# Two projections of a short convolution as seven block products, their sums on GpSimd, in a two-block network on one NeuronCore

## The chip, the core and the metric

The program runs on 1 core of one Trainium2 chip. The metric is the device time of one execution in microseconds (us). All data is float32. The engines are called by their names in the profile: PE (TensorE, matmuls) and PEld (its weight loads), DVE (VectorE), ACT (ScalarE), POOL (GpSimd), and SP, whose queue issues the weight loads from HBM. Every engine takes its instructions in the order in which they are written; semaphores order the engines among each other.

## The reference

Two blocks run one after the other. The first is a stack of two layers over 16 meta tokens and 256 real ones (272 tokens of width 1024); the second is a larger block that the change does not touch. The part of a layer that the change touches is the mixer, which projects the normalised tokens `u` with one matrix and splits the result:

```python
u = rms_norm(h, pre_g)
z = jnp.einsum("bld,de->ble", u, w_in)
q, k, v, f_logit, a_val, a_gate, sc_b, sc_c, sc_x = jnp.split(z, idx, axis=-1)
log_f = jax.nn.log_sigmoid((f_logit + b_forget).astype(jnp.float32))
y_attn = forgetting_attention(q, k, v, log_f)          # 8 heads of 64
a = a_val * jax.nn.sigmoid(a_gate)
a = causal_depthwise_conv(a, a_dw_w) + a_dw_b          # 31 taps, 256 channels
a = jax.nn.silu(layer_norm(a, a_ln_g, a_ln_b))
y_conv = jnp.einsum("blc,ce->ble", a, a_pw_w)
y_sc = sc_b * causal_depthwise_conv(sc_c * sc_x, sc_conv_w)   # 3 taps, 256 channels
y = jnp.concatenate([y_attn, y_conv, y_sc], axis=-1)
y = jnp.einsum("ble,ed->bld", head_rms_norm(y, head_g), w_out)
```

After it comes the layer's feed-forward network (FFN).

## The kernel before

Activations lie feature-major: 128 features on the partitions, 272 tokens beside each other, eight such tiles for the width of 1024 (`U` holds `u`). Weights come in strips of 1024 rows by 256 columns (1 MB), one after the other through four slots `W[0]` to `W[3]` in a written order. SP loads a strip into a slot when PE has signalled `done` of the slot's last strip; PE waits for `land` of the slot. Results are made in eight PSUM banks of 512 columns; a bank is taken with `take(b)` and freed by the engine that has read it.

In a layer's mixer PE goes through a fixed list: strips of `a_val` and `a_gate`, the query, forget and key strips, the first value strip (`values(0, i)` in three pieces), scores of heads 0 and 1 (`scores(j)`, two matmuls), the two statistics of the layer norm behind the 31-tap convolution (`stat(CV, ...)`, which waits for the semaphore `conv`, and `stat(SQ, ...)`; line 786), then the strips of `sc_c` (slot 1, in two halves, `half_slot`, line 1089), `sc_x` (slot 2, `slot_fm`, line 806), the second value strip, `sc_b`, and so on. Between them stand the transposes of the weighted scores (`turn(j)`, line 1107), the next scores (lines 1096, 1097), and the products of weights and values (`weigh(pair)`).

A strip by `slot_fm` or `half_slot` is two output tiles of eight matmuls each: 128x128 weights, 272 tokens. ACT copies each finished tile to SBUF. In float32 each written matmul is two instructions of PE in the trace.

DVE computes the 31-tap convolution of the mixer in the same time as PE runs the query, key and value strips: for each tap and each of the two channel tiles one instruction (line 2996 for the first tap, line 2998 for the other 30), with both inputs in SBUF. Behind tap 9 stand the three small instructions of the forget gate. Behind the convolution DVE takes the row minima of the scores (`mask_min`, line 3005), the mean subtraction of the layer norm, and reciprocals (`invert`), all in that order.

POOL fills constants, and in a layer's mixer it zeroes the query and key tiles (line 1842), sets ones in them (line 1912), issues two small DMAs behind the forget gate (lines 1918, 1919), copies a diagonal (line 1924), and then waits for reciprocals from DVE to scale exponentials (lines 1926, 1931, 1933).

The FFN of a layer, further on, already computes its strips by seven block products (`seven_products`, line 852): of a strip seen as 2x2 blocks (two output tiles, two halves of the 1024 rows) and the tokens as 2x2 blocks (two halves of the rows, two halves of 136 tokens), seven products of sums of blocks take the place of eight. Each product is four matmuls over 136 tokens. The sums of tokens are made once by DVE, the sums of weights for each strip by POOL (lines 1943, 1945) and DVE. ACT takes snapshots of unfinished results (line 2057), which DVE adds to the rest (lines 2949, 2953, 2959).

`p.meet` and `p.leave` only carry semaphore counts from one engine's program to another's.

## Time and profile before

| | before |
|---|---|
| time, median of 3 runs | 1957.62 us (1957.46 to 1958.21) |
| span of the profiled execution | 1956.5 us |
| instructions in it | 31965 |
| PE busy | 1935.6 us (99%) |
| DVE busy | 1276.0 us (65%) |
| ACT busy | 576.3 us (29%) |
| POOL busy | 219.5 us (11%) |
| PE's share of the chain that ended last | 94% |

The span goes from the first to the last instruction of the profiled execution; the medians of the runs stand 1.1 us above it (1957.62 - 1956.5), which is what lies around the instructions. Times in rows are microseconds from the start of the span. A timeline row is: start, duration, engine, line, operation, output<-inputs, shape, count, and in brackets the idle time of the engine before it with what ended it. Consecutive instructions of one line are merged into one row. The granted clock of PE is shown as PEclk, where 1.00 is 2.4 GHz and 0.50 is 1.2 GHz; it stands at 0.9 or more in all 40 slices of the page.

### The profile page before, as it was taken

To read this page: it belongs to the slowest core of one execution; us is meant where nothing else is said; L and a number is where in the kernel's file an instruction comes from. 1 tells how busy PE (TensorE), PEld (TensorE's weight loads), DVE (VectorE), ACT (ScalarE), POOL (GpSimd) and SP (SyncE) were. 2 spreads that over 40 slices of the span, in tenths; PEclk is the share of its full clock that TensorE was granted. 3 is DMA by queue.
4 is the path that set the end of the run, shared out by engine and by line. 5 is a ranking of instruction groups with operands and counts; after the bars stand their busy time and mean duration, and the time that the engine had idled before them with its cause. 6 is when DMAs were issued, how large, how long until landed. Compare 5 with 4: busy or idle time off the path is not lost.

```text
span 1956.5 us, 31965 instructions
## 1 busy us (share of the span) xinstructions
PE 1935.6 (99%) x12809; PEld 1755.3 (90%) x12809; DVE 1276.0 (65%) x2559; ACT 576.3 (29%) x1393; POOL 219.5 (11%) x267
## 2 busy tenths in 40 slices
PE   9999999999999999999999999999999999999998
PEld 7878999977799999888888887999998999999998
DVE  5425887572278865899768556445566776766664
ACT  3343332224533313111110003433343323132211
POOL 6100440312014200000000001001211200000000
PEclk9999999999999999999999999999999999999999
DMA  6354554353545542555545355332222224545552
GB/s 207 109 193 133 165 168 155 121 152 118 171 151 166 190 136 74 180 166 167 172 159 175 103 174 169 104 107 87 87 65 70 82 75 142 172 151 165 165 172 82
DMA packets 272109, 273.85 MB, mean 140 GB/s; under 512 B 7982, under 2 KB 269338, under 8 KB 271962
## 3 DMA queue, kind: packets, MB, share of 16 engines
q1 hardware_dynamic: 270152, 267.84, 42.9%
q0 software_dynamic: 1216, 3.32, 0.5%
q8 instruction: 102, 1.67, 0.4%
q10 hardware_dynamic: 594, 0.65, 0.1%
q14 instruction: 45, 0.37, 0.1%
HBM read 270.57 MB, written 1.08 MB: 139 GB/s over the span
## 4 chain that ended last, share of the span: by engine, by line
PE 94%; DVE 3%; ACT 1%; DMA 1%; issue 1%; ACTq 0%; DVEq 0%; SPq 0%; PEldq 0%
PE bank L852 53%; PE bank L806 8%; PE bank L1367 8%; PE bank L1586 5%; PE bank L1003 2%; PE bank L1452 2%; PE bank L1637 2%; PE bank L1730 1%; PE bank L1080 1%; PE bank L1570 1%; PE bank L1130 1%; PE bank L1692 1%; PE bank L1089 1%; PE bank L1433 1%; PE bank L1284 1%; PE bank L1278 1%
## 5 line engine op out<-in xcount | busy, mean ns | idle before, releaser
L852 PE MATMUL bank<-arena,SQ 128*128 128x136 f32 (+2 forms) x2176 | 341.4, 308 | 0.1
L852 PEld LDWEIGHTS bank<-arena,SQ 128*128 128x128 f32 x2176 | 307.0, 191 | 17.2 <-ACT arena L2057 0.3
L852 PE MATMUL bank<-arena,W 128*128 128x136 f32 (+2 forms) x1824 | 272.6, 301 | 2.7 <-issue 2.1
L852 PEld LDWEIGHTS bank<-arena,W 128*128 128x128 f32 x1824 | 247.6, 191 | 15.3 <-issue 4.1
L2057 ACT ACTIVATE H<-bank 128x128 f32<-128x128 f32 (+1 forms) x260 | 82.4, 317 | 534.3 <-PE bank L852 534.2
L852 PE MATMUL bank<-U,W 128*128 128x136 f32 (+2 forms) x1296 | 194.6, 303 | 0.0
L852 PEld LDWEIGHTS bank<-U,W 128*128 128x128 f32 x1296 | 176.4, 191 | 10.9 <-issue 2.9
L3205 DVE SCALAR_TENSOR_TENSOR W<-W,CC 128x256 f32<-128x256 f32 x280 | 128.3, 483 | 7.0
L852 PE MATMUL bank<-arena 128*128 128x136 f32 (+1 forms) x1024 | 124.1, 278 | 0.0
L852 PEld LDWEIGHTS bank<-arena 128*128 128x128 f32 x1024 | 120.6, 191 | 0.0
L806 PE MATMUL bank<-U,W 128*128 128x272 f32 (+1 forms) x512 | 118.4, 392 | 1.4 <-ACT U L2355 0.8
L806 PEld LDWEIGHTS bank<-U,W 128*128 128x128 f32 x512 | 96.8, 190 | 22.1 <-issue 2.3
L2057 ACT ACTIVATE arena<-bank 128x136 f32<-128x136 f32 x176 | 49.3, 280 | 169.3 <-PE bank L852 169.2
L852 PE MATMUL bank<-U,SQ 128*128 128x136 f32 (+2 forms) x608 | 98.2, 304 | 0.0
L852 PEld LDWEIGHTS bank<-U,SQ 128*128 128x128 f32 x608 | 85.9, 191 | 4.1
L1943 POOL TENSOR_TENSOR SQ<-W 128x512 f32<-128x512 f32 x32 | 40.8, 1275 | 268.7 <-PE bank L852 268.7
L1988 POOL TENSOR_TENSOR W<-W 128x512 f32<-128x512 f32 x32 | 42.1, 1316 | 250.4 <-PE bank L1637 105.8
L3104 DVE SCALAR_TENSOR_TENSOR arena<-arena,PL 128x270 f32<-128x270 f32 x72 | 61.8, 859 | 2.6
L1963 POOL DMA_DIRECT2D gate_rows<-arena x4 | 2.1, 542 | 528.0 <-ACT arena L2451 528.0
L2263 ACT ACTIVATE arena<-arena,PL 128x272 f32<-128x272 f32 x80 | 41.8, 522 | 64.4 <-DVE arena L2953 56.9
L852 PE MATMUL bank<-arena,U 128*128 128x256 f32 (+1 forms) x352 | 59.2, 327 | 0.4 <-DVE U L2936 0.4
L1586 PE MATMUL bank<-H,W 128*128 128x256 f32 x256 | 59.1, 380 | 0.3 <-ACT W L2545 0.3
(505 smaller groups left out, 3266.8 us busy)
## 6 DMA issues: line engine op xcount, KB each, us to landing
W<-in_ffn_w_up_dram SPq DMA_DIRECT2D x44, 1024.0 KB, 5.1
W<-in_ffn_w_in_dram SPq DMA_DIRECT2D x44, 1024.0 KB, 5.1
W<-in_ada_w_dram SPq DMA_DIRECT2D x36, 1024.0 KB, 7.1
W<-in_mix_w_in_dram SPq DMA_DIRECT2D x36, 1024.0 KB, 5.4
W<-in_ffn_w_down_dram SPq DMA_DIRECT2D x16, 1408.0 KB, 7.0
W<-in_ffn_w_out_dram SPq DMA_DIRECT2D x16, 1408.0 KB, 6.4
W<-in_w_in_dram SPq DMA_DIRECT2D x21, 1024.0 KB, 6.0
W<-in_w_out_dram SPq DMA_DIRECT2D x8, 1024.0 KB, 8.7
```

Source lines behind the costliest of these rows:

```text
L806: last = mm(bank[b][0:m, 0:n], W[r][:, kk, t * P:t * P + m], rhs(kk), start=kk == 0, stop=kk == k - 1)
L852: last = mm(o, a(k), b[:, k], start=not adds and k == 0, stop=k == kt - 1, skip_group_check=True)
L1003: return mm(bank[2 * (r % 2) + t][:, c0:c0 + n], W[r][:, k, t * P:(t + 1) * P], rhs(k), start=k == 0, stop=k == KD - 1, skip_group_check=True)
L1367: last = mm(o, x, y, start=i == 0, stop=i == n - 1 and bias is None, skip_group_check=True)
L1452: last = mm(bank[b][:, c + n * P:c + (n + 1) * P], tok[:, k, n * P:(n + 1) * P], w[:, k], start=clear and k == n == 0, stop=k == 3, skip_g ...
L1586: ins = mm(o, x, y, start=clear and k == 0, stop=k == 3, skip_group_check=True)
L1943: eng.tensor_tensor(WS[n % 2][:, 0], part(1, 0), part(1, 1), ALU.add).then_inc(S.order_pool, p.inc(S.order_pool))
L1988: eng.tensor_tensor(WSR[o], x, y, op).then_inc(S.wsum, p.inc(S.wsum))
L2057: act(sn[:, i, :], bank[b][:, c:c + w], ACT.Copy).then_inc(S.snap, p.inc(S.snap))
L2263: act(CZ[:, 2 * s + t, :], Z[:, g % 2, 2 * s + t, :], ACT.Copy, scale=PLs[l][:, c:c + 1]).then_inc(S.tap, p.inc(S.tap))
L3104: stt(CZ[:, i, 2:], Z[:, g % 2, i, 0:T1 - 2], w(0), CZ[:, i, 2:], ALU.mult, ALU.add).then_inc(sem, p.inc(sem))
L3205: ins = stt(o, x, c, o, ALU.mult, ALU.add) if k else ts(o, x, c, None, ALU.mult)
```

## The change

It touches the mixer of both layers. The strips of `sc_c` and `sc_x` are computed by seven block products (`mixed_steps`), like the FFN's strips but in two banks rather than three: both halves of a 512-column bank serve as separate accumulators. The sums that they need are all written for POOL: four sums of token blocks (`TBM_`, 128x544 each) behind the setting of ones, and four sums of weight blocks (128x512 each) for each of the two strips behind the copy of the diagonal. ACT takes four snapshots of 136 columns for each strip in place of two copies of 272 (`kept_mixed`), and DVE adds them to what the banks hold at the end (`mixed_fold`), behind the reciprocals of heads 2 and 3. ACT's SiLUs of the convolution branch, with the two table loads around them, move from behind `exps(3)` to behind `mixed(0)`, the copy of the first pair of weighted values. The pointwise weights are loaded by two DMAs into the last rows of slots 0 and 1 rather than by one into slot 0. Several semaphores are merged into `kept` and `cact`; that changes no wait.

```diff
+        TBM_ = [v[:, 4 * i:4 * i + 4, c:c + T1 // 2] for v, c in ((U, 2 * P + 32), (SQ, T1)) for i in range(2)]
+        WSA = TBU
+        WSB = [H2[:, 4 * (i // 2):4 * (i // 2) + 4, (i % 2) * P:(i % 2 + 1) * P] for i in range(4)]
+        SNM = HIB[:, SEQ:SEQ + 2 * T1].rearrange("p (i n) -> p i n", i=4)
...
-                eng.dma_start(W[0][:, KD:KD + 2, :], cols(pw, 0, k=2)).then_inc(S.land[0], p.inc(S.land[0], 16))
+                for k in range(2):
+                    eng.dma_start(W[k][:, SK - 1:SK, :], cols(pw, 0, k0=k, k=1)).then_inc(S.land[0], p.inc(S.land[0], 16))
...
+                def mixed_steps(r, o):
...
+                    eng.wait_ge(S.land[r], p.next(S.land[r], 16))
+                    take(bx)
+                    for k in range(4):
+                        add(bank[bx][:, near], raw(0, 0, k), layer_tokens(0, 0)[:, k], k, True)
+                        yield
+                    take(by)
+                    if r == 1:
+                        eng.wait_ge(S.mix_tsum, p.next(S.mix_tsum))
+                    eng.wait_ge(S.mix_wsum, p.next(S.mix_wsum))
+                    for k in range(4):
+                        add(bank[by][:, near], o[0][:, k], TBM_[0][:, k], k, True)
+                        yield
+                    eng.wait_ge(S.mix_snap, p.next(S.mix_snap))
+                    for k in range(4):
+                        add(bank[bx][:, far], raw(0, 1, k), layer_tokens(1, 0)[:, k], k, False, False)
+                        yield
+                    eng.wait_ge(S.mix_snap, p.next(S.mix_snap))
+                    for k in range(4):
+                        add(bank[by][:, far], raw(1, 1, k), TBM_[3][:, k], k, False)
+                        yield
...
+                    eng.wait_ge(S.mix_wsum, p.next(S.mix_wsum))
+                    eng.wait_ge(S.mix_snap, p.next(S.mix_snap))
+                    for k in range(4):
+                        ins = add(bank[bx][:, near], o[2][:, k], TBM_[2][:, k], k, False)
...
-                half_slot(1, 0)
+                multipliers = mixed_steps(1, WSA)
+                weave(multipliers, 16)
                 turn(0)
                 scores(2)
-                half_slot(1, 1)
+                weave(multipliers, None)
                 turn(1)
                 scores(3)
-                slot_fm(2, u1, T1)
+                weave(mixed_steps(2, WSB), None)
                 turn(2)
...
+            def mixed_sums(r, o, loads):
+
+                part = lambda t, h: W[r][:, 4 * h:4 * h + 4, t * P:(t + 1) * P]
+                eng.wait_ge(S.land[r], p.next(S.land[r], loads))
+                for i, x, y, op in ((0, part(1, 0), part(1, 1), ALU.add), (1, o[0], part(0, 0), ALU.subtract),
+                                    (3, part(0, 1), o[1], ALU.subtract), (2, part(0, 0), part(1, 0), ALU.subtract)):
+                    eng.tensor_tensor(o[i], x, y, op).then_inc(S.mix_wsum, p.inc(S.mix_wsum))
+                    eng.wait_ge(S.mix_wsum, p.now(S.mix_wsum))
...
+                eng.wait_ge(S.us, p.next(S.us, KD))
+                p.skip(S.us, KD)
+                for n, x, y in ((0, layer_tokens(0, 1), layer_tokens(0, 0)), (1, layer_tokens(1, 1), TBM_[0]),
+                                (2, layer_tokens(1, 1), layer_tokens(0, 1)), (3, layer_tokens(1, 0), TBM_[1])):
+                    sem = S.mix_tsum if n == 3 else S.order_pool
+                    eng.tensor_tensor(TBM_[n], x, y, ALU.subtract).then_inc(sem, p.inc(sem))
+                    eng.wait_ge(sem, p.now(sem))
                 eng.wait_ge(S.f_ready, p.next(S.f_ready))
...
+                p.meet(f"mixed{l}")
+                mixed_sums(1, WSA, 32)
+                mixed_sums(2, WSB, 32)
                 eng.wait_ge(S.rc, p.next(S.rc))
...
+                def kept_mixed(r, which):
...
+                    for n in which:
+                        i, src = ((0, x), (3, z), (1, x), (2, y))[n]
+                        eng.wait_ge(S.mix_prod, p.next(S.mix_prod, 2 if n == 2 else 1))
+                        act(SNM[:, i, :], src, ACT.Copy).then_inc(S.mix_snap, p.inc(S.mix_snap))
...
+                kept_mixed(1, (0, 1))
                 evict(0)
+                kept_mixed(1, (2,))
                 exps(2)
-                copies(1, SCC)
+                kept_mixed(1, (3,))
                 evict(1)
                 exps(3)
+                kept_mixed(2, range(4))
+                evict(2)
+                exps(4)
+                mixed(0)
                 for t in range(2):
                     eng.wait_ge(S.xn, p.next(S.xn))
                     act(CS[:, t, :], CV[:, t, :], ACT.Silu, bias=PLs[l][:, C_LNB + t:C_LNB + t + 1]).then_inc(S.cact, p.inc(S.cact))
                 if l == 0:
                     act(CC[:, :, 6:8], GS[:, 0, :, :], ACT.Silu).then_inc(S.cc, p.inc(S.cc))
                 tables(LOG_EXP)
-                copies(2, SCX)
-                evict(2)
-                exps(4)
-                mixed(0)
                 values(3, 1)
...
+                def mixed_fold(r, dst):
...
+                    eng.wait_ge(S.mix_snap, p.next(S.mix_snap, 4))
+                    tt(dst[:, 0, far], SNM[:, 1, :], bank[by][:, near], ALU.add).then_inc(S.order_dve, p.inc(S.order_dve))
...
+                    eng.wait_ge(S.mix_prod, p.next(S.mix_prod, 6))
+                    tt(dst[:, 0, near], SNM[:, 0, :], bank[bx][:, far], ALU.add)
...
                     invert(j % 3, 2)
+                    if j in (2, 3):
+                        r, dst = {2: (1, SCC), 3: (2, SCX)}[j]
+                        mixed_fold(r, dst)
```

The first place is POOL's program in a layer's mixer. Before, behind the zeroing of the arena tiles (`QA`, `KA`, `QC`), it stands so:

```order
L1842 MEMSET arena 128x16
L1912 AFFINE_SELECT arena<-arena 8x4x272 x2
L1918 DMA arena<-arena 8x4x272
L1919 DMA arena<-arena 8x4x272
L1924 COPY arena<-arena 128x8x16
L1926 TENSOR_SCALAR arena<-arena,RC 128x272
```

With the change the same place reads so; `U` and `SQ` hold the token sums, `W` and `H` (H2) the weight sums:

```order
L1969 AFFINE_SELECT arena<-arena 8x4x272 x2
L1978 TENSOR_TENSOR U<-U 128x4x136 x2
L1978 TENSOR_TENSOR SQ<-U 128x4x136 x2
L1982 DMA arena<-arena 8x4x272
L1983 DMA arena<-arena 8x4x272
L1988 COPY arena<-arena 128x8x16
L1957 TENSOR_TENSOR W<-W 128x512 x4
L1957 TENSOR_TENSOR H<-W 128x4x128
L1957 TENSOR_TENSOR H<-H,W 128x4x128
L1957 TENSOR_TENSOR H<-W,H 128x4x128
L1957 TENSOR_TENSOR H<-W 128x4x128
L1993 TENSOR_SCALAR arena<-arena,RC 128x272
```

Twelve instructions with two SBUF inputs have been set ahead of the scaling of exponentials, four of them ahead of the two DMAs. DVE's program in the same part of a layer is the same as before: the convolution is L2998 before and L3080 with the change, between the gate's `FM` and `FC` (8x272) and the first row minima.

The second place is PE's program from the first layer's score matrices over the strips of `sc_c` and `sc_x`. Before, with the convolution's statistic as the rows of `mean_c`:

```order
L786 MATMUL bank<-arena,mean_c 128x272 x2
L1080 MATMUL bank<-W,U 128x256 x8
L786 MATMUL bank<-SQ,mean_c 128x272 x2
L1074 MATMUL bank<-W,U 32x256 x8
L1165 MATMUL bank<-ident,arena 128x128 x2
L1167 MATMUL bank<-ident,arena 32x128 x4
L1089 MATMUL bank<-U,W 128x272 x8
L1107 MATMUL bank<-ident,arena 128x128 x3
L1096 MATMUL bank<-arena 128x128
L1097 MATMUL bank<-arena 128x256
L1089 MATMUL bank<-U,W 128x272 x8
```

With the change, from the first strip's first product on:

```order
L1102 MATMUL bank<-U,W 128x136 x12
L1102 MATMUL bank<-SQ,W 128x136 x4
L1158 MATMUL bank<-ident,arena 128x128 x3
L1147 MATMUL bank<-arena 128x128
L1148 MATMUL bank<-arena 128x256
L1102 MATMUL bank<-U,W 128x136 x8
L1102 MATMUL bank<-SQ,W 128x136 x4
```

Four products (16 matmuls) stand ahead of the first transposes and three (12) behind the next scores, where two output tiles of eight matmuls over 272 tokens stood. Everything ahead of the strip is in the same order.

## Rows read from the trace of the kernel before

**Rows 1.** The page, busy time and share by engine.

```profile
PE 1935.6 (99%) x12809; PEld 1755.3 (90%) x12809; DVE 1276.0 (65%) x2559; ACT 576.3 (29%) x1393; POOL 219.5 (11%) x267
```

**Rows 2.** Timeline of PE, first layer: start us, duration us, instruction, count.

```profile
66.90 1.08 PE L786 MATMUL bank<-arena,mean_c 128*128 128x272 f32 x4
...
74.00 3.93 PE L1089 MATMUL bank<-U,W 128*128 128x272 f32 x16
...
82.42 0.49 PE L1107 MATMUL bank<-ident,arena 128*128 128x128 f32 x3
...
83.41 7.50 PE L806 MATMUL bank<-U,W 128*128 128x272 f32 x32
```

**Rows 3.** Timeline of PE, second layer.

```profile
438.43 1.08 PE L786 MATMUL bank<-arena,mean_c 128*128 128x272 f32 x4
```

**Rows 4.** Timeline of DVE, first layer.

```profile
46.68 19.97 DVE L2998 SCALAR_TENSOR_TENSOR arena<-arena,PL 128x272 f32<-128x272 f32 x42
...
83.61 0.29 DVE L3005 CUSTOM_DVE_ANT_0 arena<-bank,mask 128x128 f32<-128x128 f32 x1 [2.67 <-PE bank L1097]
```

**Rows 5.** Timeline of DVE, second layer.

```profile
405.62 0.92 DVE L2981 TENSOR_TENSOR arena<-arena 128x272 f32<-128x272 f32 x2 [0.88 <-ACT arena L2103]
...
417.45 20.11 DVE L2998 SCALAR_TENSOR_TENSOR arena<-arena,PL 128x272 f32<-128x272 f32 x42
```

**Rows 6.** Timeline of ACT, first layer.

```profile
75.37 0.38 ACT L2140 ACTIVATE arena<-bank 128x256 f32<-128x256 f32 x1
...
85.09 0.18 ACT L2153 ACTIVATION_READ_ACCUMULATOR arena<-arena,NM 128x1 f32 x1
```

**Rows 7.** Timeline of PE, FFN of the first layer.

```profile
190.74 2.02 PE L852 MATMUL bank<-U,W 128*128 128x136 f32 x16
192.59 2.02 PE L852 MATMUL bank<-arena,SQ 128*128 128x136 f32 x16
```

**Rows 8.** The page's groups: count, busy us, mean ns of one, idle before.

```profile
L2057 ACT ACTIVATE arena<-bank 128x136 f32<-128x136 f32 x176 | 49.3, 280 | 169.3 <-PE bank L852 169.2
```

**Rows 9.** Timeline of ACT, second layer.

```profile
472.52 0.60 ACT L2139 ACTIVATE arena<-bank 128x512 f32<-128x512 f32 x1 [7.12 <-PE bank L1074]
```

**Rows 10.** Timeline of POOL, first layer.

```profile
34.36 2.44 POOL L1912 TENSOR_SCALAR_AFFINE_SELECT arena<-arena 8x1088 f32<-8x1088 f32 x2
```

**Rows 11.** Timeline of SP's queue, 52 to 55 us.

```profile
53.74 0.37 SPq L592 DMA_DIRECT2D W<-in_w_in_dram  x1
```

**Rows 12.** DMA issues: source, count, size each, median us from issue to landing.

```profile
W<-in_w_in_dram SPq DMA_DIRECT2D x21, 1024.0 KB, 6.0
```

**Rows 13.** Timeline of POOL, FFN of the first layer.

```profile
204.05 1.27 POOL L1943 TENSOR_TENSOR SQ<-W 128x512 f32<-128x512 f32 x1 [3.69 <-PE bank L852]
205.40 1.35 POOL L1945 TENSOR_TENSOR SQ<-W 128x512 f32<-128x512 f32 x1
210.53 1.27 POOL L1943 TENSOR_TENSOR SQ<-W 128x512 f32<-128x512 f32 x1 [3.79 <-PE bank L852]
```

**Rows 14.** Timeline of DVE, the same stretch.

```profile
204.56 1.06 DVE L3101 SCALAR_TENSOR_TENSOR arena<-arena,PL 128x271 f32<-128x271 f32 x1
205.66 1.39 DVE L3104 SCALAR_TENSOR_TENSOR arena<-arena,PL 128x270 f32<-128x270 f32 x1
207.08 0.50 DVE L3101 SCALAR_TENSOR_TENSOR arena<-arena,PL 128x271 f32<-128x271 f32 x1
...
211.12 0.44 DVE L2959 TENSOR_TENSOR arena<-arena,bank 128x272 f32<-128x272 f32 x1
```

**Rows 15.** Timeline of DVE, 35.8 to 36.1 us.

```profile
35.74 1.35 DVE L2998 SCALAR_TENSOR_TENSOR arena<-arena,PL 128x272 f32<-128x272 f32 x1
```

**Rows 16.** Timeline of PE, end of the program.

```profile
1949.67 0.42 PE L1812 MATMUL bank<-ident,arena 128*128 128x128 f32 x2
```

**Rows 17.** Windows: us, busy of PE, PEld, DVE, ACT, POOL, PEclk, DMA share, GB/s.

```profile
1953.00:1956.50 3.50, 0.00 (x0) 0.00 (x0) 0.00 (x0) 0.00 (x0) 0.00 (x0) 0.55 0.74 276
```

**Rows 18.** Timeline of PE, start of the program.

```profile
2.84 4.61 PE L757 MATMUL bank<-ident 128*128 128x128 f32 x20 [2.84 <-POOL LNT L1851]
```

More of the change, by code:

```diff
@@ L1186, in _ @@
                 scores(5)
-                eng.wait_ge(S.land[0], p.next(S.land[0], 16))
+                eng.wait_ge(S.land[0], p.next(S.land[0], 32))
                 slot_fm(0, u1, T1)
@@ L2212, in _ @@
                 exps(5)
[L2213 removed]
+                copies(0, SCB, S.kept)
                 evict(4)
```

83 lines of the change are left out of this document (55 added, 28 removed).

## The prediction

> **What bounds the kernel now.** I read the page first: PE is busy 99% of the span, DVE 65%, POOL 11% [rows 1]. PE's one long pause is the first 2.84 us of the program [rows 18]. So every microsecond of work that PE loses is a microsecond of time, and any wait that another engine puts in front of PE costs as much, unless there is slack. Then I laid the timelines of PE, DVE and POOL around the two strips beside each other. In the first layer PE comes to the first statistic of the convolution (`stat(CV)`) at 66.90 [rows 2], and DVE's last 42 taps run from 46.68 for 19.97 us, to 66.65 [rows 4]. The convolution is done 0.25 us before PE asks for it. In the second layer PE comes at 438.43 [rows 3] and the taps end at 417.45 + 20.11 = 437.56 [rows 5]: 0.87 us. PE shows no wait there, and yet DVE's convolution is all but critical: it runs some 30 us without a pause under PE's strips. Everything that follows on DVE (row minima, layer norm, reciprocals) stands behind it.
>
> **The strips themselves.** A strip before is 32 instructions of PE over 272 tokens (16 written matmuls) and lasts 7.50 us with the drain of the last [rows 2]. Seven products of four matmuls over 136 tokens are 56 instructions. The FFN runs them already: 16 last 2.02 us, but the next begins after 192.59 - 190.74 = 1.85 [rows 7], so the drain is 0.17 and the pace 0.116 each. A strip goes from 7.50 - 0.17 = 7.33 us to 56 x 0.116 = 6.48. The gain is 0.85 us a strip, 3.4 us for four.
>
> The snapshots give part of that back. The third product may begin only when ACT has copied the first. In the first strip PE starts at 74.00 [rows 2] and is through two products at 75.85. ACT is busy with the value copies until 75.37 + 0.38 = 75.75 [rows 6], then needs 0.28 for a snapshot [rows 8] and, my estimate, 0.15 for two handovers: PE goes on at about 76.2, a wait of 0.35. In the second strip, count from the first transpose behind the first strip (82.42 before). PE begins the strip 83.41 - 82.42 = 0.99 us later and wants the first snapshot 1.85 us after that, at 2.84; ACT ends `exps(3)` at 85.09 + 0.18, which is 2.85 [rows 2, 6], and the snapshot is there at about 3.2: again 0.35. DVE's folds do not add to this: `mask_min(3)` begins 83.61 - 82.42 = 1.19 us after the transpose [rows 2, 4], and the three adds of a fold fit ahead of it. Two waits of 0.35 in each of two layers are 1.4 us. The strips are worth 3.4 - 1.4 = 2.0 us.
>
> The moved SiLUs cost nothing: they and their two table loads land in a stretch in which ACT sits idle for 7.12 us ahead of the second value copy [rows 9]. If that cover were too short, `evict(3)` and with it the transposes of head 4 would be late next. The second DMA for the pointwise weights costs nothing: the rows that it fills are free, and the wait for slot 0 comes behind the second value strip.
>
> **The sums on POOL, and what they meet.** When do the twelve run? In the first layer POOL is done with line 1912 at 34.36 + 2.44 = 36.8 [rows 10], so the four token sums run from there, some 6 us. The strip of `sc_x` is issued at 53.74 [rows 11], that of `sc_c` one strip of 7.33 us before, at 46.4, and each lands some 6.0 us later [rows 12]: POOL makes their sums from about 52.5 to 58.5 and from 59.7 to 65.7. All twelve lie between 36.8 and 66.65, under the convolution. In the second layer the first token sum can start as soon as `U` is written, which is before DVE's pause of 0.88 us ahead of 405.62 [rows 5]; the other eleven meet line 2981 or the taps behind it. POOL itself has the time: its next instruction, the first scaling, needs a reciprocal that DVE makes only behind the convolution.
>
> What does DVE pay for a tensor operation of POOL beside it? The FFN shows it. POOL's two sums start at 204.05 and 205.40 [rows 13]. DVE's `scalar_tensor_tensor` instructions, of the same kind as the taps, last 0.50 us alone, 1.06 beside the first sum and 1.39 beside the second; from start to start it is 205.66 - 204.56 = 1.10 and 207.08 - 205.66 = 1.42 [rows 14], where alone it would be 0.53 (0.50 and the handover). So a sum of 128x512 costs DVE 0.57 us where DVE comes upon it midway and 0.89 where both queue without a pause. The taps are not exempt: the one that starts at 35.74 lasts 1.35 us [rows 15], beside line 1912 on POOL [rows 10], where the later ones come every 19.97 / 42 = 0.475 us [rows 4]. In the mixer both engines queue without a pause, so I take 0.89 for each weight sum and, scaled by 544/512, 0.95 for each token sum. First layer: 8 x 0.89 + 4 x 0.95 = 10.9 us. Second layer, with three token sums, the first of them in part in DVE's own pause (0.3 us less, an estimate): 8 x 0.89 + 3 x 0.95 - 0.3 = 9.7 us.
>
> The Trainium skill, page "SBUF — State Buffer", section "Who interferes with whom", speaks against this change: a DVE instruction with two SBUF inputs contends with a GpSimd instruction that reads SBUF, and the one that comes second is blocked until the other is through. The trace agrees in kind (1.39 us in place of 0.50) but shows less than the 1.27 us that the sum lasts. Taken to the letter, the rule gives the time of the second rival below.
>
> PE cannot cover it. Its list puts `stat(CV)` ahead of the next value pieces, so it stands still for 10.9 - 0.25 = 10.65 us in the first layer and for 9.7 - 0.87 = 8.8 us in the second, 19.5 us together. What is behind the statistic (minima, exponentials, transposes) keeps its distances and only shifts.
>
> **The clock.** PE has no pause of this length within its work. But behind its last matmul, at 1949.67 + 0.42 = 1950.09 [rows 16], the granted clock falls: its mean over 1953.00 to 1956.50 is 0.55 [rows 17], so it was full for the first 0.35 us and half (1.2 GHz) for the rest, and fell 3.3 us after the work ended. A pause of 9 to 11 us should then end at the lower clock. What that costs is seen at the start: 20 instructions over 128 columns last 4.61 us, 0.23 each [rows 18], where 136 columns take 0.116 later [rows 7]. Half of 4.61 is lost, 2.3 us, and I take that for each pause: 4.6 us. The bounds are 0 (the clock stays) and twice that.
>
> **The sum.** 1957.6 - 2.0 (strips) + 19.5 (pauses) + 4.6 (clock) = 1979.7 us. It is made on the span of the profiled execution (1956.5, so 1978.6 with the change) and carries over to the median, which lies 1.1 us above that span.
>
> **Rivals.**
> - *The convolution is not held up*: only the strips count, 1955.6 us, or 1954.2 without the snapshot waits. For it: beside the sum at 210.53 an add of 272 columns with one input in PSUM lasts its plain 0.44 us [rows 13, 14], so the two engines can live together, and no row shows a tap beside a tensor operation of POOL. Against it: the taps have both inputs in SBUF, like the instructions that were held up. This is the rival on the other side; it needs the loss for each sum to stay under (0.25 + 0.87 + 2.0) / 23, about 0.14 us. 8%.
> - *A sum holds DVE for its whole length*: 23 x 1.28 = 29.4, less the slack of 1.1, gives 28.3; 1957.6 - 2.0 + 28.3 + 4.6 = 1988.5 us. For it: both queues are denser than anywhere in the trace. Against it: 0.89 at the densest place there is. 15%.
> - *Only the lighter price*: each sum costs 0.57, as the first of the FFN's pair. 23 x 0.57 - 1.1 = 12.0 us of pauses, each longer than 3.3: 1957.6 - 2.0 + 12.0 + 4.6 = 1972.2 us. 13%.
> - *The clock stays at full*: 1957.6 - 2.0 + 19.5 = 1975.1 us. 12%.
> - *The forecast* as summed, within 1975.5 and 1985: 52%.
>
> **How the numbers follow.** Faster by over 0.2% means under 1953.7 us, slower by over 0.2% over 1961.5; that is about what a measurement of this kernel can tell from no change. The first rival falls between the two almost wholly (0.06), with 0.02 for faster; all others are slower, 0.92. The range leaves out the first rival and reaches from below the light price to the full block: 1970 to 1989.
>
> **What the profile of the changed kernel would show.** If right: most taps still last 0.50 us, but about 22 of the 120 last 1.3 to 1.5 us, each beside a sum on POOL; the taps end near 77.5 and 447 us; PE waits for DVE at `stat(CV)`, some 10.6 and 8.8 us, its two longest waits; PEclk falls to 0.5 behind each of them. The strips: 56 instructions of about 0.116 us, with two waits for ACT's snapshots of 0.2 to 0.5 us in each layer. If the taps end by 67 and 438 us, the step that failed is the price of a sum on DVE; if PE waits but resumes at full pace, it is the clock; if the waits within the strips are above 1 us, it is the snapshots. The forecast is wrong as a whole if POOL's sums run outside the convolution.

## The result: 1986.2 us, 1.4% slower

The changed kernel takes 1986.19 us (median of 4 runs, 1983.52 to 1988.67) against 1957.72 us (1957.46 to 1958.21) for the kernel before: ratio 1.0144, 95% interval 1.013 to 1.0159. The forecast was 1979.7 with a range of 1970 to 1989. The profiled execution of the changed kernel is the longest of its four, 1988.67 us with a span of 1986.9; the spread of 5 us over these four, where the four of the kernel before spread over 0.75, will need a reason too.

The page of the changed kernel, busy time by engine, beside [rows 1]:

```profile
PE 1941.8 (98%) x12905; PEld 1762.8 (89%) x12905; DVE 1302.4 (66%) x2571; ACT 576.5 (29%) x1401; POOL 251.7 (13%) x291
```

PE has 96 matmuls more and DVE 26 us more of busy time, though its 12 added instructions are short: it was made to wait inside its own instructions. What PE waited for (us in total, times, longest):

```profile
PE bank L792 <- DVE arena L3080: 20.2, 2, 11.2
PE bank L1400 <- DVEq L3310: 4.7, 4, 2.2
PE bank L763 <- POOL LNT L1899: 2.8, 1, 2.8
```

The first line is the statistic of the convolution, foreseen. The second, in the second block, was not. The third stands in the kernel before as well. PE's timeline around the strips, first layer (line 1102 is the products), beside [rows 2]:

```profile
78.18 2.15 PE L792 MATMUL bank<-arena,mean_c 128*128 128x272 f32 x4 [11.25 <-DVE arena L3080]
80.13 5.44 PE L1090 MATMUL bank<-W,U 128*128 128x256 f32 x16
...
88.14 3.46 PE L1102 MATMUL bank<-U,W 128*128 128x136 f32 x24
91.44 1.09 PE L1102 MATMUL bank<-SQ,W 128*128 128x136 f32 x8
92.36 0.49 PE L1158 MATMUL bank<-ident,arena 128*128 128x128 f32 x3
...
103.00 1.09 PE L1102 MATMUL bank<-SQ,H 128*128 128x136 f32 x8
103.93 0.27 PE L1158 MATMUL bank<-ident,arena 128*128 128x128 f32 x1
```

and in the second layer, beside [rows 3]:

```profile
460.45 2.15 PE L792 MATMUL bank<-arena,mean_c 128*128 128x272 f32 x4 [8.93 <-DVE arena L3080]
```

DVE's last 42 taps, first layer and second, beside [rows 4, 5]:

```profile
50.66 27.79 DVE L3080 SCALAR_TENSOR_TENSOR arena<-arena,PL 128x272 f32<-128x272 f32 x42
...
433.17 27.54 DVE L3080 SCALAR_TENSOR_TENSOR arena<-arena,PL 128x272 f32<-128x272 f32 x42
```

POOL's sums in the first layer (four of tokens, eight of weights):

```profile
36.85 2.83 POOL L1978 TENSOR_TENSOR U<-U 128x544 f32<-128x544 f32 x2 [0.18 <-POOL arena L1969]
39.76 2.92 POOL L1978 TENSOR_TENSOR SQ<-U 128x544 f32<-128x544 f32 x2
...
53.19 5.53 POOL L1957 TENSOR_TENSOR W<-W 128x512 f32<-128x512 f32 x4
58.90 1.26 POOL L1957 TENSOR_TENSOR H<-W 128x512 f32<-128x512 f32 x1 [0.19 <-DMA W<-in_w_in_dram]
```

The reader is to see three things. POOL's sums run where they were placed, 36.85 to 64.4, all under the convolution. Four of them push the start of the last 42 taps from 46.68 to 50.66, 3.98 us or 1.00 each; eight more stretch those taps from 19.97 to 27.79, 7.82 us or 0.98 each (second layer 27.54 - 20.11 = 7.43, 0.93 each). Instruction by instruction, 99 of the 120 taps last about 0.5 us. The other 21 last 1.35 to 1.77 us: the first of them beside line 1969 of POOL, as in the kernel before [rows 15], and 20 beside a sum. The four token sums of the second layer end at 422.6, ahead of its first tap (423.1): they meet the two instructions of line 3063 and the two of 3078, which take 2.82 and 1.65 us, where the kernel before has 0.92 and 0.75. And the four matmuls of the statistic take 2.15 us where [rows 2] has 1.08. Windows (columns as in [rows 17], PEclk third from the end) say why:

```profile
78.20:83.80 5.60, 5.60 (x13) 4.42 (x14) 3.07 (x16) 3.23 (x12) 1.64 (x3) 0.50 0.01 3
85.40:92.00 6.60, 6.46 (x60) 4.86 (x59) 1.00 (x2) 2.92 (x9) 0.92 (x1) 1.00 0.51 159
461.00:466.00 5.00, 5.00 (x13) 3.90 (x12) 2.54 (x15) 3.23 (x12) 1.58 (x3) 0.50 0.01 3
```

(The first two numbers of a window row are its ends, in us; then come its length and the busy time of PE, PEld, DVE, ACT and POOL.) Behind each pause PE works at half its clock (1.2 GHz), from 78.18 to 83.8 and from 460.45 to 466.1, and then at full again.

**The account.** Where an unchanged instruction of PE starts in the two traces, first behind both layers, then through the second block:

```
before us   after us   later by
   855.9      879.8      23.82
   880.9      906.0      25.08
   905.8      931.7      25.92
   931.2      957.8      26.54
   933.7      963.9      30.23
  1949.8     1980.3      30.49
```

The two layers cost 23.8 us: 20.2 of pauses, 5.7 of clock, less 1.9 for the strips (a sum of 24.0). Another 6.7 us are lost between 880 and 966 us, in code that the change does not touch. PE waits there for sums that DVE makes of modulation weights, 4.7 us in four waits, and DVE is late because it waits for a weight strip of the FFN (DVE and PE, the same turn of that loop):

```profile
871.66 0.69 DVE L2969 TENSOR_TENSOR SQ<-W 128x512 f32<-128x512 f32 x1 [1.75 <-DMA W<-in_ffn_w_in_dram]
...
881.34 0.64 PE L1400 MATMUL bank<-W,ONE 128*32 128x256 f32 x8 [1.19 <-DVEq L3310]
```

Most of the rest is the clock once more. Behind the last and longest of the four waits it is at half from 961.0 to 964.4, and 16 matmuls take 5.41 us where the kernel before takes 3.72, 1.7 us more. PE's timeline and a window of the changed kernel, and the same matmuls before:

```profile
960.32 0.64 PE L1400 MATMUL bank<-W,ONE 128*32 128x256 f32 x8 [2.19 <-DVEq L3310]
960.89 5.41 PE L862 MATMUL bank<-U,W 128*128 128x256 f32 x16
```
```profile
961.00:964.40 3.40, 3.40 (x9) 2.65 (x10) 3.04 (x5) 0.00 (x0) 0.00 (x0) 0.51 0.90 294
```
```profile
932.09 3.72 PE L852 MATMUL bank<-U,W 128*128 128x256 f32 x16
```

These 6.7 us are those of the profiled execution, which is 2.5 us above the median of the four; in the others the second block may well lose less.

### The profile page after: what moved, and what is told of

It is laid out like the page before. It is cut to its first block, busy times and chain, and to the rows that moved or that the text cites. A ratio compares the mean times of both kernels' runs of the same rounds, so it can differ in the third digit from the quotient of the medians.

```text
span 1986.9 us, 32217 instructions
## 1 busy us (share of the span) xinstructions
PE 1941.8 (98%) x12905; PEld 1762.8 (89%) x12905; DVE 1302.4 (66%) x2571; ACT 576.5 (29%) x1401; POOL 251.7 (13%) x291
## 3 DMA queue, kind: packets, MB, share of 16 engines
HBM read 270.57 MB, written 1.08 MB: 137 GB/s over the span
## 4 chain that ended last, share of the span: by engine, by line
PE 85%; DVE 10%; DMA 2%; ACT 2%; issue 1%; DVEq 0%; POOL 0%; ACTq 0%; POOLq 0%
PE bank L862 48%; PE bank L1419 8%; PE bank L816 5%; PE bank L1638 4%; DVE arena L3080 4%; PE bank L1013 2%; PE bank L1504 2%; PE bank L1689 2%; PE bank L1181 1%; PE bank L1778 1%; PE bank L1622 1%; DVE W L3306 1%; DMA W<-in_ffn_w_in_dram 1%; PE bank L1090 1%; PE bank L1744 1%; PE bank L1102 1%
## 5 line engine op out<-in xcount | busy, mean ns | idle before, releaser
L862 PEld LDWEIGHTS bank<-U,W 128*128 128x128 f32 x1296 | 177.6, 191 | 11.5 <-issue 2.9
L816 PE MATMUL bank<-U,W 128*128 128x272 f32 (+1 forms) x448 | 103.4, 392 | 1.4 <-ACT U L2437 0.8
L816 PEld LDWEIGHTS bank<-U,W 128*128 128x128 f32 x448 | 84.6, 190 | 19.6 <-issue 2.3
L3080 DVE SCALAR_TENSOR_TENSOR arena<-arena,PL 128x272 f32<-128x272 f32 x120 | 75.3, 669 | 2.1
```

The lines of the kernel that those rows point to most:

```text
L816: last = mm(bank[b][0:m, 0:n], W[r][:, kk, t * P:t * P + m], rhs(kk), start=kk == 0, stop=kk == k - 1)
L862: last = mm(o, a(k), b[:, k], start=not adds and k == 0, stop=k == kt - 1, skip_group_check=True)
L3080: ins = stt(CV[:, t, :], src, w, CV[:, t, :], ALU.mult, ALU.add)
```

## The experiments

Eleven kernels. The reasons to test were: a sum of POOL holds DVE up when both read SBUF; the clock is a cost of its own; the strips are worth 2 us; and for the 6.7 us a theory that is set out behind the fourth run. The kernel before ran again beside them (1957.59, 1957.63 and 1957.94 us), and each ratio is to it.

### Without the sums

POOL makes none of its twelve sums; PE's products read raw blocks in their place (the last one the identity), so that the two projections are not those of the reference.

```diff
-                    eng.tensor_tensor(o[i], x, y, op).then_inc(S.mix_wsum, p.inc(S.mix_wsum))
+                    eng.sem_inc(S.mix_wsum, p.inc(S.mix_wsum))
...
-                        add(bank[by][:, near], o[0][:, k], TBM_[0][:, k], k, True)
+                        add(bank[by][:, near], raw(1, 0, k), layer_tokens(0, 1)[:, k], k, True)
```

> The twelve tensor operations of POOL in each layer's mixer are left out (POOL only signals); the seven products read unsummed blocks of weights and tokens (the last one the identity), so the two projections are not those of the reference. Everything else is the changed kernel. Theory A (POOL's sums hold up DVE's taps, PE waits for the convolution, and its clock falls): the taps end near 66.7 and 437.5 us, PE has no wait at the statistic, and only the strips count: 1957.7 - 2.0 = 1955.7 us, within 1954 to 1957. Rival B (the loss lies in the strips themselves, their snapshots, folds or bank waits): it stays near 1986. Rival C (the second block lost some 7 us through something the change did to the loads, not through the delay): some 1962 us.

1959.67 us (1958.68 to 1963.34, 10 runs), ratio 1.0014 (1.0005 to 1.0023). PE's timeline:

```profile
67.11 1.08 PE L792 MATMUL bank<-arena,mean_c 128*128 128x272 f32 x4
...
74.22 4.38 PE L1102 MATMUL bank<-U,W 128*128 128x136 f32 x32
...
90.01 0.49 PE L1158 MATMUL bank<-ident,arena 128*128 128x128 f32 x3
```

No wait at the statistic, no half clock, and the two strips with what lies between last 90.01 - 74.22 = 15.79 us, as in the changed kernel (103.93 - 88.14 = 15.79). Pauses and clock hang on the sums. But the kernel does not come out below the one before, as was expected: PE is 2.2 us ahead of it at the entry of the second block and 1.4 behind at the end, so the second block loses 3.6 us, most of it at the same line 1400.

### The sums, with plain strips

The opposite half: POOL makes all sums, PE computes `sc_c` and `sc_x` with `half_slot` and `slot_fm`.

```diff
-                multipliers = mixed_steps(1, WSA)
-                weave(multipliers, 16)
+                eng.wait_ge(S.mix_tsum, p.next(S.mix_tsum))
+                eng.wait_ge(S.mix_wsum, p.next(S.mix_wsum, 4))
+                half_slot(1, 0)
...
-                weave(mixed_steps(2, WSB), None)
+                eng.wait_ge(S.mix_wsum, p.next(S.mix_wsum, 4))
+                slot_fm(2, u1, T1)
```

> POOL's twelve sums in each layer stay, at the same places, and PE waits for them, but the two strips are again eight plain products over 272 tokens, with ACT's copies and without DVE's folds. Theory A: the same two pauses of 11.2 and 8.9 us at the statistic and the same clock loss of some 5.7 us; the strips no longer give their 2 to 3 us: 1957.7 + 20.2 + 5.7 = 1983.6, plus what the second block loses (0 to 7 us, as it falls), so 1984 to 1990. Rival B: 1958 to 1962.

1982.92 us (1981.52 to 1984.02), ratio 1.0129 (1.0114 to 1.0144). What PE waited for at the statistic:

```profile
PE bank L792 <- DVE arena L3091: 20.2, 2, 11.2
```

The same 20.2 us to the digit, so the products do not make the pauses. The program is 24.0 us later at the end and as late already ahead of the second block, which loses nothing; the expectation of at least 1984 lay above the time because it added a clock loss of 5.7 us, where 4.4 were lost (6.70 + 6.42 - 2 x 4.37). Oddly, a kernel with the slower strips is faster than the changed one, by 6.5 us on the spans of the profiled executions (1986.9 against 1980.4) and 3.3 by the medians. The spans: 6.7 us of the second block, and 1.3 of the clock (from the first statistic to the second PE takes 6.70 and 6.42 us here, 7.23 twice in the changed kernel and 4.37 in the one before), less 1.9 for the strips, 6.1 of the 6.5. At the entry of the second block the two kernels stand within 0.2 us of each other (23.8 and 24.0 us behind the kernel before), and one loses 6.7 us there and the other nothing: the delay as such is not what costs.

### Writes in place of sums

Plain strips again, and each sum of POOL is two `memset` of the same tile: POOL is busy in the same places and only writes.

```diff
-                    eng.tensor_tensor(o[i], x, y, op).then_inc(S.mix_wsum, p.inc(S.mix_wsum))
+                    eng.memset(o[i], 0.0).then_inc(S.order_pool, p.inc(S.order_pool))
+                    eng.wait_ge(S.order_pool, p.now(S.order_pool))
+                    eng.memset(o[i], 0.0).then_inc(S.mix_wsum, p.inc(S.mix_wsum))
```

> As plain_strips, but each sum of POOL is replaced by two memsets of the same place, which write SBUF and read nothing, so POOL is busy about as long in the same stretch. Theory A in its narrow form (what holds DVE's two-input instructions up is that POOL reads SBUF): no tap lasts over 0.6 us beside a memset, no pause, 1957 to 1959 us. Rival D (any work of POOL on SBUF holds DVE up): a loss in proportion to POOL's busy time, 1970 to 1990 us.

1957.45 us (1956.83 to 1957.86, 10 runs), ratio 0.9999 (0.999 to 1.0009). DVE's last 42 taps, and one of POOL's writes beside them:

```profile
46.40 19.94 DVE L3096 SCALAR_TENSOR_TENSOR arena<-arena,PL 128x272 f32<-128x272 f32 x42
```
```profile
53.22 0.52 POOL L1972 MEMSET W<- 128x512 f32 x1
```

No tap is held up (19.97 us in [rows 4]). What costs is not POOL's writing, nor its instructions or semaphores; what the sums do beyond that is read SBUF. Reads without writes were not tried.

### The clock kept up

38 matmuls of 128 columns ahead of each statistic, where PE stands still anyway.

```diff
+                take(7)
+                keep_busy(bank[7][:, 0:P], 38)
+                eng.sem_inc(S.free[7], 1)
                 stat(CV, T1, True, 2, b=7, ready=S.conv, full=S.ln_full, lhs=mean_c)
```

> The changed kernel with 38 extra matmuls of 128 columns on PE, into the bank of the statistic, ahead of the statistic in each layer: some 8.4 us of work at full clock, which fits into the pauses of 11.25 and 8.93 us. Theory A: the pauses as such stay, the clock does not fall, and the 2.85 + 2.8 us that PE ran at half pace come back: 5.7 us less than the changed kernel, about 1980.5. Rival E (the clock falls anyway, or costs nothing): no change. If the second block's loss is a matter of when its loads land, it will change by some microseconds with the shift, in either direction.

1977.89 us (1977.73 to 1978.89), ratio 1.0103 (1.0086 to 1.012). PE's timeline and a window (columns as above):

```profile
69.90 8.65 PE L803 MATMUL bank<-mean_d,ident 128*128 128x128 f32 x76
80.25 1.16 PE L792 MATMUL bank<-arena,mean_c 128*128 128x272 f32 x4 [1.70 <-DVE arena L3083]
```
```profile
80.00:86.00 6.00, 5.75 (x32) 4.68 (x36) 3.34 (x17) 3.41 (x13) 1.76 (x3) 1.00 0.00 0
```

The clock stays full, and the statistic is followed by the strip after 87.43 - 80.25 = 7.18 us, where the changed kernel takes 88.14 - 78.18 = 9.96 and [rows 2] 7.10. The half clock costs the changed kernel 2.86 us a pause (9.96 - 7.10). This kernel is 8.3 us faster than the changed one by the medians and 9.7 by the spans. Of these, 5.6 are the clock (9.96 - 7.18 = 2.78 in the first layer and as much in the second) and 6.7 the second block, which loses nothing here; some 2.6 are given back, 2.1 of them ahead of the first statistic (80.25 against 78.18), where the clock was at half from 9.9 to 16.7 us. Why would the second block lose nothing?

### The theory of the fetches

Queue 8 of the profile carries instructions (the other such queue, 14, has packets of another size). Its line on the page of the changed kernel:

```profile
q8 instruction: 103, 1.69, 0.4%
```

103 packets of 16 KB; PE has 2 x 12905 = 25810 instructions with its weight loads, so one packet for each 250, and with the 568 that its sequencer handles alone (waits and increments, by the trace) 26378, one for each 256. Before has 102. In the second block they come some 26 us apart, and the loads of FFN strips that DVE's sums wait for come every 25 to 26 us. Start of each fetch in the second block, from the packets of that queue, and of those loads with the time to landing:

```
kernel            fetches us                     loads us (us to landing)
before            860.8 886.6 911.9 937.9        866.2 (5.13) 891.1 (5.17) 916.5 (5.11) 941.5 (5.26)
after             865.1 891.3 917.9 944.3        865.1 (6.56) 891.3 (6.14) 917.0 (5.84) 943.1 (7.55)
no_sums           839.2 865.5 891.4 917.5        839.0 (6.64) 865.3 (5.64) 890.6 (5.64) 916.4 (6.88)
plain_strips      859.6 884.7 910.0              865.2        890.2        915.1        (all about 5.0)
keep_clock        856.5 881.4 908.2 933.1        861.9 (5.21) 886.9 (5.07) 911.8 (4.94) 937.2 (4.97)
```

In `after` and `no_sums` the fetch falls on the issue of the load or up to 1.2 us behind it, and the load lands 0.5 to 2.4 us late; in the others the fetch starts 3.6 to 5.6 us ahead of it. All 13 traces agree. Between 825 and 975 us they hold 77 such loads with a recorded landing: the 19 with a fetch that starts between issue and landing (0 to 4.3 us behind the issue) land after 5.21 to 7.55 us, 17 of them after more than 5.6, and the other 58 after 4.85 to 5.52. The change adds 192 instructions of PE (96 matmuls, 96 weight loads). The 38 written fillers of a layer add 152, those of both layers 304, so that `keep_clock` has 496 more than the kernel before: nearly two whole distances between fetches, which puts them back beside the loads as before. The theory (F in the expectations): how many instructions PE has run decides on which load a fetch falls; the second block loses where they meet. Its rival is that the content of the change (sums, order, late transfers) reaches into the second block.

### 64 idle increments at the start of the changed kernel

```diff
+            for _ in range(64):
+                eng.sem_inc(S.pad, 1)
             eng.wait_ge(S.consts, p.next(S.consts))
```

> The changed kernel with 64 idle instructions more in PE's program (increments of a semaphore that nobody waits for), at its very start, where PE waits for POOL's constants. In the changed kernel's trace the second block lost 6.7 us because four weight strips (issued at 865.1, 891.3, 917.0 and 943.1) landed after 5.8 to 7.6 us instead of 5.1, and a 16 KB fetch of PE's instructions (queue 8) stands at 865.1, 891.3, 917.9 and 944.3. Theory F (the fetches, one for about every 256 instructions of PE, here some 26 us apart like the strips, fall upon the strips' loads, and the change moved them there with its 192 more instructions): 64 more instructions move each fetch some 6.5 us ahead, between the loads; the second block's waits on DVE go, 1980 to 1981 us, with a narrower spread. Rival G (the loss comes with the seven products or with the shift in time as such): 1984 to 1988 as before.

1984.37 us (1983.6 to 1985.53), ratio 1.0134 (1.0119 to 1.0149). PE's waits:

```profile
PE bank L795 <- DVE arena L3083: 14.3, 2, 8.9
PE bank L766 <- issue: 12.6, 1, 12.6
```

The increments were no idle matter: they begin at 2.7 us and the 64 take 9.7, 0.15 each, so that the first matmul comes at 12.6 and not at 2.8; most of that is taken back at the first statistic, where the wait is 5.3 us and not 11.25. PE enters the second block 1.6 us later than in the changed kernel and loses nothing there (landings 5.04 to 5.25), as F says. The total is 1.8 us below the changed kernel by the medians, 5.1 by the spans, but above the 1980 to 1981 expected: the increments were taken to cost nothing.

### 192 increments where none was lost

The counter-test: plain strips, which had no loss, with the number of instructions that the products add, 96 in each pause.

```diff
+                for _ in range(96):
+                    eng.sem_inc(S.pad, 1)
                 stat(CV, T1, True, 2, b=7, ready=S.conv, full=S.ln_full, lhs=mean_c)
```

> plain_strips (the sums on POOL, the strips as plain products, 1982.9 us, no wait in the second block) with 96 idle instructions of PE in each layer, inside the long pause at the statistic, where they cost nothing: 192 in all, as many as the seven products add. Theory F: the fetches fall upon the loads as in the changed kernel, and the second block loses 3 to 7 us: 1986 to 1990. Rival G: 1982.9.

1991.85 us (1990.29 to 1994.37), ratio 1.0173 (1.0158 to 1.0188). PE's waits:

```profile
PE bank L793 <- issue: 24.8, 2, 12.4
PE bank L1416 <- DVEq L3321: 4.8, 4, 1.3
```

The increments again cost more than the pause holds (PE stands still for 12.4 us each time, in place of 11.2 and 9.0), and the total lies above the 1986 to 1990 expected. But the wait in the second block is there, without a single product: 4.8 us, four times, and PE loses 5.0 us between its entry and its end. Fetches at 872.5 and 898.7 meet loads at 872.4 and 898.5, and two more, at 928.2 and 955.6, start 3.6 and 4.3 us behind loads at 924.6 and 951.3; the four land after 6.42 to 6.72 us. This run carries most for F.

### The sums moved out from under the convolution

All the work of the changed kernel. POOL makes the weight sums behind the convolution, around its first scalings; DVE makes the token sums behind its reciprocals.

```diff
-                mixed_sums(1, WSA, 32)
-                mixed_sums(2, WSB, 32)
+                eng.wait_ge(S.conv, p.next(S.conv, 2))
+                mixed_sums(1, WSA, 32, (0, 1))
...
+                    if j == 1:
+                        mixed_sums(1, WSA, 32, (2, 3))
+                        mixed_sums(2, WSB, 32)
```

> The changed kernel with the sums where DVE has no convolution to run: POOL waits for the end of the convolution and makes two weight sums of the first strip ahead of the first scaling and the other six behind the scalings of heads 0 and 1; DVE makes the four token sums itself behind the reciprocals of heads 0 and 1. The work is the whole of the changed kernel's. Theory A: no pause at the statistic, no fall of the clock, the strips give their 2 us; PE's instruction stream is that of the changed kernel, so by theory F the second block loses what it lost in no_sums, some 3.5 us: about 1959.5. If DVE's token sums meet POOL's scalings and come late, the first strip waits up to 1 us in each layer: up to 1961.5. Rival G would have 1956 to 1958.

1961.23 us (1957.98 to 1964.3, 10 runs), ratio 1.0016 (1.0006 to 1.0025). 25 us of the loss are gone: no pause, no half clock, and the program is 2.1 us ahead of the kernel before at the entry of the second block, which is what the strips bring. The second block gives away 3.1 us; PE's wait:

```profile
PE bank L1400 <- DVEq L3313: 2.9, 3, 1.6
```

With the 64 increments at its start:

> later_sums with the 64 idle instructions of PE at the start of the program. Theories A and F together: no pause, no fall of the clock, no fetch upon the loads: 1957.6 - 2.0 = 1955.6 us, within 1954.5 to 1957.5, and 3 to 4 us below later_sums. Rival G: the same as later_sums.

1965.06 us (1964.48 to 1965.96, 6 runs), ratio 1.0037 (1.0024 to 1.0049). The second block keeps its length (landings 5.04 to 5.22 us), and the six runs lie within 1.5 us of each other, where the ten of `later_sums` lie within 6.3. But nothing takes back what the increments cost: the first statistic comes 8.8 us later (75.56 against 66.76), so that the total missed the 1955.6 expected. A cheaper way to shift the count was needed.

### Narrow matmuls in place of increments

Matmuls of 4 columns behind the warm-up; one written is four instructions of PE.

```diff
+            for _ in range(16):
+                mm(bank[4][0:4, 0:4], ident[:, 0:4], ident[:, 0:4], start=True, stop=True, skip_group_check=True)
```

16 in the changed kernel:

> The kernel after with 16 narrow matmuls (4 columns, 64 more instructions of PE) behind the warm-up at the start. Theory F: the fetches move a quarter of their distance off the loads, the second block keeps its length (no shift beyond that of the two layers), and the kernel is faster than after by 6.7 us less the cost of the narrow matmuls (1 to 3 us): 1980 to 1983 us. Pauses at the statistic and the half clock behind them as in after. Rival: the second block's loss belongs to the change and stays: 1987 to 1989 us.

1981.42 us (1980.33 to 1982.32), ratio 1.0117 (1.0103 to 1.0131). PE's timeline at the start, and the issues of 860 to 950 us in `before`, `after` and this kernel (count, size, median us to landing):

```profile
7.11 0.94 PE L765 MATMUL bank<-ident 128*4 128x4 f32 x32
```
```profile
W<-in_ffn_w_in_dram SPq DMA_DIRECT2D x7, 1024.0 KB, 5.1
```
```profile
W<-in_ffn_w_in_dram SPq DMA_DIRECT2D x7, 1024.0 KB, 6.4
```
```profile
W<-in_ffn_w_in_dram SPq DMA_DIRECT2D x7, 1024.0 KB, 5.0
```

They take 0.9 us and hide ahead of a load: the matmul that waits for it starts at 9.58 us, in the changed kernel at 9.56. Set against the trace of the changed kernel, PE is 1.2 us earlier at the entry of the second block (the two stretches at half clock cost 3.7 us here, from statistic to statistic 5.93 and 6.48) and 7.9 earlier at the end: the 6.7 us of the profiled execution are back, by 64 instructions that compute nothing. By the medians the gain is 4.8 us (1986.19 - 1981.42).

51 in the kernel before, meant to put its own fetches on its loads:

> The kernel before with nothing but 51 narrow matmuls (4 columns, 204 more instructions of PE) behind the warm-up at the start of the program. Theory F (the second block's loss is PE's own instruction fetches falling on the issue of the FFN strips' loads; which load they meet is set by how many instructions PE has run): 204 instructions are 0.8 of the 256 between two fetches, so the fetch at 886.6 comes at about 866, on the load at 866.2, and so do the following ones. The second block, untouched, then loses 3 to 7 us of PE (its waits for DVE at the modulation sums), on top of what the narrow matmuls cost at the start (at 0.02 to 0.1 us for each of 102 instructions 2 to 10 us), which shows in the first block. Rival: the loss in the second block comes from the changed content of the first (another order of DVE or POOL, a late transfer): then the second block keeps its length here to 0.5 us.

1963.44 us (1962.4 to 1965.21, 8 runs), ratio 1.0026 (1.0016 to 1.0037). In the profiled execution 2.8 us are lost ahead of the second block (the matmuls, and an early dip of the clock) and only 1.5 in it, under the 3 that F asked for. The fetches at 869.4, 895.2 and 920.9 meet loads at 869.0, 894.9 and 920.2; these land after 6.27, 5.21 and 5.82 us. The sign is right and the wait at the modulation sums is there:

```profile
PE bank L1350 <- DVEq L3211: 1.3, 2, 0.9
```

but a meeting is not always paid for. The profiled execution is also the fastest of the eight; by the median, 5.5 us above the kernel before, the loss in the second block would be about 2.7 if what is ahead of it costs 2.8 in every run (an estimate; no other run has a trace).

16 in the kernel with the later sums:

> later_sums (POOL's weight sums behind the convolution, the token sums on DVE) with 16 narrow matmuls (4 columns, 64 more instructions of PE) at the start. Theory F: its second block then loses nothing, and the time is that of later_sums less about 3 us plus the 1 to 3 us of the narrow matmuls: 1958 to 1961 us, with the second block's length that of the kernel before. If the narrow matmuls cost under 1 us, 1957 or a little under and so at the kernel before. Rival: the loss stays, 1962 to 1964 us.

1956.3 us (1955.98 to 1958.64, 11 runs), ratio 0.9991 (0.9983 to 1.0): 1.6 us under the kernel before and the lowest median of all, though its interval reaches up to no change. The second block keeps its length (PE is 1.6 us ahead at its entry and at its end), where `later_sums`, with the same work, lost 3.1 us. DVE's taps, 19.97 us as in the kernel before, and POOL's weight sums behind them:

```profile
47.32 19.97 DVE L3080 SCALAR_TENSOR_TENSOR arena<-arena,PL 128x272 f32<-128x272 f32 x42
```
```profile
67.37 2.62 POOL L1961 TENSOR_TENSOR W<-W 128x512 f32<-128x512 f32 x2 [17.99 <-DVE arena L3080]
```

## Why the prediction came out as it did

- **The convolution is held up, and PE with it: right.** 20 long taps of 120 beside a sum were seen where about 22 were forecast, pauses of 11.25 and 8.93 us where 10.65 and 8.8 were. A sum cost DVE 0.93 to 1.00 us, not 0.89 and 0.95. The Trainium skill, page "SBUF — State Buffer", section "Who interferes with whom", has DVE's two-input instructions contend with a GpSimd instruction that reads SBUF and not with one that only writes. The runs agree on both: 0.93 to 1.00 us for each sum, none for the writes. A sum cost DVE less than its own length in the changed kernel, though, 1.38 us (5.53 / 4), so that the second rival's full block was not reached.
- **The clock: right in kind, a fifth short in this execution.** 2.3 us a pause were forecast, 2.86 measured for each (7.23 - 4.37, from statistic to statistic). The 2.3 came from the pace of the first 20 matmuls alone: the profile of the kernel before gives their stretch (0 to 5 us) a granted clock of 1.00, so no row shows that they ran at half clock, and that the figure came near is partly luck. The same pauses cost 2.33 and 2.05 us with plain strips and 1.56 and 2.11 in the changed kernel with narrow matmuls: it depends on how long PE works before its clock comes back, 5.6 us in the changed kernel, 4.6 with plain strips and 3.0 with narrow matmuls (first layer). Taken over these three, the forecast is about the mean.
- **The strips: right.** 16.74 us before (83.41 + 7.50 - 0.17 - 74.00 by [rows 2, 7]) against 15.79, 0.95 us a layer for 1.0. The waits for snapshots, 0.7 us a layer by forecast, are 0.6: the trace has four in both layers, 1.2 us in all. With the short waits that the strips had before as well, the first strip's first four products take 0.5 us more than 32 instructions of 0.116 (92.36 - 88.14 = 4.22) and the second strip 0.3 (6.82 for 56).
- **SiLUs and the split load: right**, no wait of PE names them.
- **The sum: a term is missing.** On the spans: 1956.5 - 1.9 + 20.2 + 5.7 = 1980.5, and 1986.9 was measured. The 6.4 us between are the second block (4.7 of waits, 1.7 of clock), to which the forecast gave no term. Of the two things that the forecast said of added instructions, their duration and their place, neither is what matters there: 192 more of them move every later fetch of PE's code by three quarters of the distance between two, onto the loads for which DVE waits. That is shown from both sides, by 192 instructions without products (the loss appears) and by 64 more on top of the change (it goes). The spread fits: the kernels with the meeting vary by 2.8 to 6.3 us from run to run (`before_narrow51` 2.8, `plain_pad192` 4.1, `no_sums` 4.7, `after` 5.2, `later_sums` 6.3), the changed kernels without it by 1.0 to 2.7 (`memsets` 1.0, `keep_clock` 1.2, `later_pad64` 1.5, `after_pad64` 1.9, `after_narrow16` 2.0, `plain_strips` 2.5, `later_narrow16` 2.7). It is not shown, since the kernel before, without the meeting, has single runs up to 4.2 us above its lowest in one set of 15. The total lay within the range because the range held the full block of the second rival, that is by luck and not by its reason: 1981.42 us, `after_narrow16` without the meeting, is what belongs beside the forecast of 1979.7.
- **Open:** why a fetch makes a load land late. The Trainium skill, page "Runtime: NRT & Kernel Launch", section "Instruction fetch mechanics", has a sequencer fetch its code in blocks of 256 instructions over a DMA queue of its own, at a cost that is mostly hidden. The 256 instructions a packet agree; the cost is hidden where a fetch falls between loads, and 1.5 to 6.7 us a run where it does not. The traces narrow it down a little: the first packet on the loads' queue comes 1.02 to 1.05 us behind the issue in all 77 cases, met or not, so a late load does not start late. What holds its end is not shown. Nor is it known why some meetings cost nothing: in `before_narrow51` the load at 894.9 lands after 5.21 us, and in `memsets`, `plain_strips`, `keep_clock` and `later_narrow16` a load between 987 and 1016 us is met and lands after 6.9 to 7.9 us, without PE losing anything. Between 1720 and 1870 us the effect is smaller too: a fetch 0.3 to 0.6 us behind the issue goes with landings of 5.15 to 5.72 us.

## What to carry to other kernels

Before work is given to an idle GpSimd, see what DVE does beside it: if both read SBUF and DVE's instructions have two inputs there, each 1.4 us tensor operation took about 1 us from DVE here, and it belongs behind DVE's critical run, not under it. A pause that this causes was paid a second time in the clock (1.6 to 2.9 us). And when code that was not touched gets slower, or the runs spread, look at when the instruction fetches fall against the loads on the critical path, and shift them with a few narrow matmuls where PE waits anyway before anything else is concluded from a difference of a few microseconds.

## What the runs showed of the hardware

- Where a fetch of PE's code (16 KB, 0.9 to 2.4 us) started with the load of a 1 MB strip or up to 4.3 us behind it, the load landed after 5.2 to 7.6 us (19 loads between 825 and 975 us), elsewhere after 4.9 to 5.5 (58 loads); the second block lost 1.5 to 6.7 us in the kernels with such meetings.
- An increment of a semaphore on PE's own queue takes 0.15 us (64 in 9.7 us, 96 in 14.8); a narrow matmul of 4 columns is four instructions and 0.06 us (16 in 0.94).
- Behind a pause of 9 to 11.5 us PE lost 1.6 to 2.9 us at half its clock, in three kernels; behind one of 5.3 us (`after_pad64`) 1.8 (6.13 - 4.37), and behind one of 2.2 us in the second block of the changed kernel 1.7.
- The 102 narrow instructions of the 51 case kept PE busy without a gap from 6.7 us on, and yet its clock dipped to half from 9.4 to 16.2 us. The kernel with 38 fillers dips there too (9.9 to 16.7 us), and so does the one with 192 increments (10.9 to 17.7), though their programs start as the others do; PE had waited 2.25 and 1.70 us for a load just ahead of the dip, where the kernel before, without a dip, waits 1.11. Why was not tried.
